# Column sums of the output projection's squares: fifteen elementwise additions on GpSimd and two TensorE products, in place of sixteen products

## The reference, cut to what matters

```
def _rmsnorm(x, g):
    xf = x.astype(jnp.float32)
    y = xf * lax.rsqrt(jnp.mean(xf * xf, axis=-1, keepdims=True) + EPS)
    return (y * g.astype(jnp.float32)).astype(x.dtype)
...
    out = jnp.concatenate([o, y], axis=-1) @ p['w_out']
...
    s = s + g_a * _rmsnorm(out, p['norm_post_mix'])
```

## Time and profile before

| | us |
|---|---|
| median of 3 runs | 1735.39 |
| the three runs | 1732.19, 1737.31, 1735.39 |
| span of the profiled execution (first to last instruction) | 1732.4 |
| TensorE busy in it | 1669.5 (96%) |
| VectorE busy | 1155.7 (67%) |
| ScalarE busy | 733.5 (42%) |
| GpSimd busy | 116.2 (7%) |
| output stage, fourteen tiles and their column sums | about 842 to 931 |

### The profile page before, as it was taken

How to read it: one execution, slowest core, us unless ns; L and a number is a source line. 1 busy time by engine, 2 the same in 40 slices (tenths; PEclk the granted TensorE clock), 3 DMA queues, 4 the chain that set the end, 5 groups by cost and what they waited for, 6 DMA issues and landing times.

```text
span 1732.4 us, 27586 instructions
## 1 busy us (share of the span) xinstructions
PE 1669.5 (96%) x10466; PEld 1445.3 (83%) x10466; DVE 1155.7 (67%) x1694; ACT 733.5 (42%) x1181; POOL 116.2 (7%) x215
## 2 busy tenths in 40 slices
PE   5998999999999999999999999999999999999998
PEld 1255999898999999999998788888888888788786
DVE  3635788788888888677777655555555555655665
ACT  1445353534535353532435544444444444343341
POOL 1001010101110010000100000000000000111110
PEclk9998999999999999999999999999999999999999
DMA  9985343442533443422896244554444546877772
GB/s 374 391 360 210 108 157 130 133 159 86 178 129 128 145 138 132 169 75 97 294 350 231 101 176 184 194 194 191 174 176 186 194 194 212 265 240 252 264 244 101
DMA packets 79011, 334.11 MB, mean 193 GB/s; under 512 B 7931, under 2 KB 20278, under 8 KB 52482
## 3 DMA queue, kind: packets, MB, share of 16 engines
q1 hardware_dynamic: 58080, 257.97, 40.3%
q0 software_dynamic: 19600, 68.25, 12.1%
q10 hardware_dynamic: 1234, 6.57, 1.0%
HBM read 328.56 MB, written 4.19 MB: 192 GB/s over the span
## 4 chain that ended last, share of the span: by engine, by line
PE 89%; DVE 4%; ACT 3%; DMA 3%; issue 1%; DVEq 0%; POOL 0%; ACTq 0%; POOLq 0%
PE o L473 10%; PE g L480 10%; PE o L475 9%; PE o L474 9%; PE o L480 9%; PE g L481 5%; PE o L481 5%; PE g L564 3%; PE g L559 2%; DVE w_lo L454 2%; PE g L567 2%; PE g L487 2%; DMA w_mod_raw<-in_w_mod_t 2%; PE o L487 2%; PE g L489 2%; PE g L488 2%
## 5 line engine op out<-in xcount | busy, mean ns | idle before, releaser
L454 DVE TENSOR_TENSOR w_lo<-w_raw,w_hi 128x2048 fp32r<-128x2048 f32 (+1 forms) x207 | 465.6, 2249 | 232.3 <-ACT w_hi L448 231.1
L448 ACT CAST w_hi<-w_raw 128x2048 fp32r<-128x2048 f32 (+1 forms) x208 | 390.2, 1876 | 343.0 <-PE o L475 182.9
L473 PE MATMUL o<-h_hi,w_hi 128*128 128x256 f32 (+1 forms) x896 | 298.6, 333 | 0.8 <-DVE w_lo L454 0.8
L475 PE MATMUL o<-h_hi,w_lo 128*128 128x256 f32 (+1 forms) x896 | 281.9, 315 | 0.0
L474 PE MATMUL o<-h_lo,w_hi 128*128 128x256 f32 (+1 forms) x896 | 281.6, 314 | 0.0
L480 PE MATMUL g<-h_hi_lo,w_hi 128*128 128x512 f32 x704 | 249.7, 399 | 0.0
L480 PE MATMUL o<-h_hi_lo,w_hi 128*128 128x512 f32 x688 | 245.0, 399 | 2.0 <-DVE h_hi_lo L1943 2.0
L481 PE MATMUL g<-h_hi_lo,w_lo 128*128 128x256 f32 x704 | 197.7, 281 | 0.0
L481 PE MATMUL o<-h_hi_lo,w_lo 128*128 128x256 f32 x688 | 193.2, 281 | 0.0
L475 PEld LDWEIGHTS o<-h_hi,w_lo 128*128 128x128 f32 x896 | 170.8, 191 | 11.4
L473 PEld LDWEIGHTS o<-h_hi,w_hi 128*128 128x128 f32 x896 | 171.3, 191 | 10.2 <-issue 3.3
(11 more groups left out here) (376 smaller groups left out, 2857.0 us busy)
## 6 DMA issues: line engine op xcount, KB each, us to landing
w_raw<-in_w_ff_t SPq DMA_DIRECT2D x88, 1024.0 KB, 6.1
w_raw<-in_w_heads_t SPq DMA_DIRECT2D x56, 1024.0 KB, 4.8
w_mod_raw<-in_w_mod_t SPq DMA_DIRECT2D x32, 1024.0 KB, 10.4
w_raw<-in_w_down_t SPq DMA_DIRECT2D x32, 1024.0 KB, 5.2
w_mod_piece_h<-in_w_mod_t POOLq DMA_DIRECT2D x112, 256.0 KB, 4.0
w_raw<-in_w_out_t SPq DMA_DIRECT2D x16, 1024.0 KB, 8.3
w_mod_tile_o<-in_w_mod_t POOLq DMA_DIRECT2D x16, 1024.0 KB, 9.4
w_mod_piece_d<-in_w_mod_t POOLq DMA_DIRECT2D x64, 256.0 KB, 5.4
```

The source lines that it names most:

```text
L448: e.copy(whi[p.split[j]][:, :n], raw[p.raw[j]][:, :n]).then_inc(hi_ready, 1)
L454: e.tensor_tensor(wlo[p.split[j]][:, :n], raw[p.raw[j]][:, :n], whi[p.split[j]][:, :n].bitcast(F32), ALU.subtract).then_inc(lo_ready, 1)
L473: e.matmul(o, a, xh, start=first, stop=False)
L475: return e.matmul(o, b, xh, start=False, stop=last)
```

## The change

The squares of output tiles 0 to 14 are added into a new buffer `o_sq_sum` on GpSimd, one tile at a time: a copy for tile 0 and fourteen additions of 128x256. In GpSimd's queue the work on tile t-3 stands behind the issue of load t (t = 3 to 15), and the last two behind load 15. ScalarE's wait for a free `o_sq` buffer is now a wait for GpSimd. TensorE no longer runs a product between output tiles; behind the last tile and the two keep-warm products it runs one product on `o_sq_sum` and one on the square of tile 15. `root_guess` waits for a new semaphore that the second of them sets. Semaphore `out_sq_used` has changed its meaning: GpSimd sets it. The line numbers of the changed kernel are higher by 2 to 17.

```diff
+        osum = at("o_sq_sum", 169, [P, SEQ])
...
             def out_tile(j):
                 tile_ready(pe, W, 0, j)
                 pe.wait_ge(wo_free, j + 3)
+                pe.wait_ge(wo_sq, j + 1)
                 for k in range(KT_N):
                     last = mm3(pe, O[j % 2][:, :SEQ], W.split[j], k, mh[:, k], ml[:, k], k == 0, k == KT_N - 1)
                 last.then_inc(w_used, 1)
-                sum_squares(j + 1, (j + 1) % 2, False)
-
-            def sum_squares(m, u, first, last=False):
-
-                pe.wait_ge(wo_sq, m + 1)
-                pe.matmul(G[0][:, :SEQ], ONES, osq[:, u], start=first, stop=last).then_inc(wo_sum, 1)
+
+            def sum_squares():
+
+                pe.wait_ge(wo_sum, KT_N - 1)
+                pe.matmul(G[0][:, :SEQ], ONES, osum[:], start=True, stop=False)
+                pe.wait_ge(wo_sq, KT_N)
+                pe.matmul(G[0][:, :SEQ], ONES, osq[:, 1], start=False, stop=True).then_inc(wo_rows, 1)
...
-            sum_squares(0, 0, True)
             for j in range(W.n):
                 out_tile(j)
             sums = [macc_o[:, n] for n in range(4)]
             keep_warm(2)
-            sum_squares(KT_N - 1, 1, False, True)
+            sum_squares()
...
-            def root_guess(summed, sums):
-
-                act.wait_ge(summed, KT_N)
+            def root_guess(summed, n, sums):
+
+                act.wait_ge(summed, n)
...
-                    root_guess(wo_sum, G[0])
+                    root_guess(wo_rows, 1, G[0])
...
+            def add_squares(m):
+
+                g.wait_ge(wo_sq, m + 1)
+                if m == 0:
+                    last = g.tensor_copy(osum[:], osq[:, 0])
+                else:
+                    g.drain()
+                    last = g.tensor_tensor(osum[:], osum[:], osq[:, m % 2], ALU.add)
+                last.then_inc(wo_sum, 1)
...
                 g.dma_start(mtile_o[t % 2][:].rearrange("p (c f) -> p c f", c=2), by_pairs[k // 2, k % 2][:, c:c + 2])\
                     .then_inc(mtile_landed[t % 2], 16)
+                if t >= 3:
+                    add_squares(t - 3)
+            add_squares(KT_N - 3)
+            add_squares(KT_N - 2)
```

More of the change, by code:

```diff
@@ L323, in build @@
         wo_free, wo_sq, wo_sum, post1 = sem("out_bank_free"), sem("out_sq"), sem("out_sq_used"), sem("res_done")
+        wo_rows = sem("out_sq_rows")
         r_ln, r_exp, r_done, h2_s = sem("rms2_log_ready"), sem("rms2_first_ready"), sem("rms2_ready"), sem("h2_scaled")
@@ L1372, in _ @@
                 res_squares(k, k + 1)
-            root_guess(s2_sum, G[3])
+            root_guess(s2_sum, KT_N, G[3])
             h2_scaled(8, 12)
```

## The result

| | before | after |
|---|---|---|
| median, us | 1733.79 (4 runs, 1730.21 to 1737.31) | 1756.36 (4 runs, 1754.17 to 1758.98) |
| ratio of the times, 95% interval | | 1.0152 [1.0117, 1.0186] |
| span of the profiled execution | 1732.4 | 1752.5 |
| first modulation piece of the output stage to the last pieces | 94.6 | 126.1 |
| first modulation piece to the modulation (`mod<-g,bmod`) | 101.8 | 133.9 |

The changed kernel is slower by 22.6 us, against a forecast of 0.5 us faster. The stage that was changed grew by 32.1 us in the profile. The feed-forward phase, which the change does not touch, came out 9.2 us shorter in that one execution. "The stage" with one number is the way from that piece to the modulation.

A forecast was written before the change was run, and what follows sets the result against it. Bound: a loop of modulation loads and VectorE, at about TensorE's pace. -6.0 us on TensorE, +4.3 in waits for low parts, +1.2 for the last load: -0.5 us, 1735.39 to 1734.9 us; range 1730.0 to 1740.0.

The forecast's parts named there:

- What bounds the kernel: Output stage: modulation loads and VectorE form a loop at its own pace, and TensorE has about the same pace.
- -6.0 on TensorE, +4.3 in waits for low parts, +1.2 for the last load: Output stage: fourteen column sums fewer save 6.0 us; TensorE's low-part waits and VectorE's last-load wait leave 0.5 us.
- ScalarE: Square of tile m waits for the addition of tile m-2; costs nothing, with 4.6 us of cover in the tightest case.
- GpSimd's additions: Fifteen on GpSimd, 0.70 us each (0.43 to 1.28), fit between two loads in 4.25 to 4.75 us idle; cost nothing.
- The end of the stage: After the last output tile: keep-warm and two column sums take the same 1.3 us as before; cost nothing.
- The rule that speaks against the change: Two-input VectorE instructions and SBUF-reading GpSimd instructions exclude each other; an addition holding VectorE up would lengthen the load loop.
- The second rival: Additions mildly hinder VectorE, 0.70 us where no load wait hides it: 2.4 us on the loop, 1737.3 us; chance 0.24.
- The first: Rival: loads speed up as TensorE does, so the whole 6.0 us gain comes through, 1729.4 us; chance 0.06.
- The third: Rival: in GpSimd's queue additions delay the next load and VectorE 0.70 us on fourteen tiles: +9.3 us, 1744.7; chance 0.07.

The follow-up runs named there:

- experiment 3: Kernel before the change, without fourteen of sixteen column sums and ScalarE's waits for them, nothing in their place: 1732.39 us, ratio 0.9988.
- experiment 5: Kernel before the change, with a third buffer for the output stage's modulation loads: 1732.34 us against 1733.52, ratio 0.9995.
- experiment 6: Changed kernel with the additions on VectorE, no drain, and a third modulation load buffer: 1728.08 us, ratio 0.9979; repeated, 1726.45 us, ratio 0.9965.
- experiment 1: Changed kernel with GpSimd's drain ahead of each addition replaced by a semaphore wait for the addition before: 1734.81 us against 1733.21, ratio 0.9997.
- experiment 2: Kernel before the change, with only a GpSimd drain added behind each modulation load's issue from the fifth on: 1741.60 us against 1733.21, ratio 1.0043.
- experiment 8: The changed kernel run again unaltered, for more runs and a second profile: 1762.35 us, ratio 1.017.

## Why the prediction was wrong, step by step

**What bounds the kernel: held.** That modulation loads and VectorE form a loop with TensorE's own pace is what experiments 3, 5 and 6 show. Less work on TensorE alone brings nothing (102.3 against 101.8 us), a third buffer alone 1.1 us, both together 6.6 us.

**-6.0 on TensorE, +4.3 in waits for low parts, +1.2 for the last load: held where it could be seen.** In experiment 3, which takes nothing but the column sums away, TensorE's waits at the start of tiles grow from 1.1 to 4.6 us, by 3.5 against the 4.3 of the sum, and VectorE waits 1.53 us for the last load's landing against 1.2. In experiment 1, the change without its drain, the time is unchanged (0.9997), and that wait is 0.42 us. In the changed kernel itself none of these waits appears; they were swallowed by the larger one.

**The failed step is the pair "ScalarE" and "GpSimd's additions".** It said that "an addition fits between two loads", at 0.43 to 1.28 us each, and "cost nothing; the cover is those 4.6 us". The price counted the addition and left out the instruction ahead of it. The diff has `g.drain()` ahead of every addition, and it got neither a price nor a bound. The order of GpSimd's queue does not show it. Its row `L2038 ISA` is another instruction, which stands once, ahead of the first addition, and costs nothing:

```profile
L2038 POOLq MODIFY_POOL_CONFIG  x2: 11/11/11, 860.7 to 860.7; - x2
```

The drain holds up GpSimd 5.2 to 9.9 us, 70.2 us in eleven times, since it stands behind the issue of a load and ends with that load's landing. That alone exceeds the cover of 4.6 us. The stage had no drain on GpSimd before, but the trace before has one at the program's end, directly behind the issue of GpSimd's last load and with no computation near it (GpSimd over time, and the drain's row in ns):

```profile
1688.66 0.54 POOL L2067 DMA_DIRECT2D w_mod_piece_d<-in_w_mod_t  x1 [0.31 <-issue]
```

```profile
L152 POOLq DRAIN  x1: 12027/12027/12027, 1688.8 to 1688.8; - x1
```

That load of 256 KB landed 8.7 us after its issue, at 1697.4, and the drain took 12.0 us, to 1700.8; what it waited for in the last 3.4 us stays open. This row says that a drain behind a load isn't free. The upper end could be read from the earlier trace rows: a load's time from issue to landing, up to 15.3 us. With a ring that allows one load in flight, that end would have stood in the range as a rival on the slow side.

**The end of the stage, "cost nothing": wrong as a consequence.** ScalarE over time in the changed kernel:

```profile
956.36 0.38 ACT L1340 ACTIVATE o_sq<-o 128x256 f32<-128x256 f32 x1 [6.09 <-POOL o_sq_sum L2038]
...
956.89 1.91 ACT L450 CAST w_hi<-w_raw 128x2048 fp32r<-128x2048 f32 x1
958.69 1.91 ACT L450 CAST w_hi_extra<-w_raw 128x2048 fp32r<-128x2048 f32 x1
960.49 0.40 ACT L1340 ACTIVATE o_sq<-o 128x256 f32<-128x256 f32 x1
```

The square of tile 14 waits 6.09 us for the drain of the last load, and two casts that had been hidden now stand ahead of the square of tile 15. TensorE over time waits for both (last, a column sum of the kernel before in the same view):

```profile
956.85 0.60 PE L909 MATMUL g<-squares 128*128 128x128 f32 x4
958.11 0.70 PE L903 MATMUL g<-o_sq_sum,squares 128*128 128x256 f32 x2 [0.66 <-POOL o_sq_sum L2038]
960.94 1.22 PE L905 MATMUL g<-o_sq,squares 128*128 128x256 f32 x2 [2.13 <-ACT o_sq L1340]
```

```profile
930.20 0.60 PE L901 MATMUL g<-o_sq,squares 128*128 128x256 f32 x2
```

The last product of the last tile ends at 957.01, and from there to the last pieces it is 966.02 - 957.01 = 9.0 us, where it was 5.17. The first column sum took 0.70 us at a granted clock of 1.00. The second took 1.22 us, twice the 0.60 of before: the granted clock was 0.50 there (960.9 to 962.2), the level of 1.2 GHz, after TensorE had stood 2.13 us waiting for the square.

**The rule that speaks against the change: it holds, and costs little here.** An addition takes 0.72 to 0.73 us when VectorE stands idle, 1.72 us beside the pieces and up to 2.37 us beside low parts, and the pieces grow from 2.66 to 2.95 us. In the row of 870.19 the first piece runs from 870.03 to 871.31 and the addition ends at 871.90, again 0.6 us later. In experiment 1 one addition comes first (918.71): the low part that starts 0.28 us into it takes 2.63 us, not 2.29. The Trainium skill (SBUF — State Buffer, Who interferes with whom) states that the two exclude each other for the whole instruction. The trace agrees in that an addition doesn't get done beside VectorE's instruction. The second rival put the price at 0.70 us on VectorE for each; measured are 0.3 us. The skill's ratio (GPSIMD Engine Reference, Performance versus the Vector engine) gave an estimate of 0.84 us for the addition by itself; measured are 0.73 us.

**The rivals.** The first (6.0 us faster) did not come, for the reason given there. The second is near to what experiment 1 shows (+1.5 us in the stage, and no difference in the times). The third named the right place, GpSimd's queue with the next load behind the addition, and the right sign. Its mechanism (shutting out by VectorE, 0.70 us a tile) was not the one that cost, and its 0.70 us are less than a third of the 2.5 us (8.6 less 6.1) by which the loads came later, each, with the drain and the addition in their way.

## What to carry to other kernels

Price every instruction that a change adds to a queue, waits and drains first. Read them from the diff, since the views of order and time leave drains out, and look for one anywhere in the trace before. A drain on an engine that also issues loads can wait for the load in flight: order two dependent instructions there by a semaphore of the first. And before work is taken from the engine that the chain names, find the loop that runs at the same pace: here a third load buffer and the moved column sums each brought at most 1.1 us, and together 6.6 us.

## What was not expected of the hardware

- GpSimd's drain ends with the landing of GpSimd's own last load, whatever SyncE has in flight: the addition behind it starts 0.2 us after that landing in ten of twelve cases and 0.5 us in two. The longest wait was 14.1 us (experiment 2). With no load of its own in flight the drain costs 0.17 us.
- An addition of 128x256 on GpSimd that starts while a VectorE instruction with two SBUF inputs is running ends 0.6 us behind it, so it takes 0.73 to 2.4 us by the place where it falls.
- The feed-forward phase has two paces, 477.0 or 486.2 us (within 0.1) in all thirteen profiles, in profiles of the same kernel too: the changed kernel had both, and so had the kernel of experiment 6. The granted clock is 1.00 in either. Window 1100 to 1300 us, of the kernel before, of the changed one, and of the changed one in experiment 8:

```profile
1100.00:1300.00 200.00, 200.00 (x1133) 173.37 (x1133) 109.99 (x107) 91.01 (x108) 0.00 (x0) 1.00 0.47 182
```

```profile
1100.00:1300.00 200.00, 200.00 (x1157) 176.34 (x1156) 112.53 (x110) 90.46 (x109) 0.00 (x0) 1.00 0.48 189
```

```profile
1100.00:1300.00 200.00, 200.00 (x1135) 173.47 (x1134) 109.61 (x107) 90.81 (x107) 0.00 (x0) 1.00 0.48 189
```

TensorE is busy throughout and gets through 1157 products, or 1133 to 1135. Over the whole page its 512-column products have a mean of 391 ns in the changed kernel's first profile and 399 ns before. What chooses the pace stays open; no experiment was aimed at it. It is large enough to be a part of why single runs of one kernel lie 10 us apart, but the runs without a profile don't tell their pace. With such a scatter a difference of a few us needs ten runs or more of each.
